# Plain fp32 for the first 36 blocks of U, GpSimd's low parts of U from block 36 on, and one-hots with the expert index innermost

## The reference

```python
q = (xt @ w_q).reshape(n_tok, PEER_HEADS, PEER_DKEY)
s1 = einsum('thd,nd->thn', q[..., :half], sub_k1); s2 = ...   # 128 keys each
v1, i1 = lax.top_k(s1, 16); v2, i2 = lax.top_k(s2, 16)
cand_s = (v1[..., :, None] + v2[..., None, :]); cand_i = i1 * 128 + i2
top_s, pos = lax.top_k(cand_s, 16); idx = take_along_axis(cand_i, pos)
g = softmax(top_s)
u = take(u_tab, idx); act = gelu(einsum('chkd,cd->chk', u, x))
out = einsum('chk,chkd->cd', g * act, take(v_tab, idx))
```

## Time and profile before

| | us |
|---|---|
| median of 3 runs | 2933.95 (2921.36 to 2942.88) |
| the profiled execution | 2944.07, span 2942.2 |
| PE busy | 2668.6 (91%) |
| DVE busy | 1974.5 (67%) |
| POOL busy | 1425.9 (48%) |
| ACT busy | 851.6 (29%) |
| outer products, L903, 2048 records | 934.6 |
| split hidden blocks and queries, L628 to L630 | 2059.3 |
| builds, L886, 3072 records | 281.9 |
| low parts on POOL, L502, 268 | 698.1 |

### The profile page before, as it was taken

How to read it: one execution, slowest core, us unless ns; L and a number is a source line. 1 busy time by engine, 2 the same in 40 slices (tenths; PEclk the granted TensorE clock), 3 DMA queues, 4 the chain that set the end, 5 groups by cost and what they waited for, 6 DMA issues and landing times.

```text
span 2942.2 us, 38986 instructions
## 1 busy us (share of the span) xinstructions
PE 2668.6 (91%) x14882; PEld 1975.3 (67%) x14882; DVE 1974.5 (67%) x3947; ACT 851.6 (29%) x1471; POOL 1425.9 (48%) x840
## 2 busy tenths in 40 slices
PE   6788769988999999999969996999799999999995
PEld 2655559978845577766647665998784456677663
DVE  2446446998657767767663445599875776677666
ACT  2356534442200022222234633354220001222222
POOL 3647545991254434445545803499214443344552
PEclk9899889998999999999979967999899999999998
DMA  6475423774599978889944802377459997788994
GB/s 239 120 162 157 150 65 111 214 240 143 186 395 370 325 276 289 298 316 371 351 147 116 230 8 67 102 203 241 147 161 380 383 322 278 267 312 295 372 359 162
DMA packets 223699, 686.36 MB, mean 233 GB/s; under 512 B 32827, under 2 KB 65995, under 8 KB 223002
## 3 DMA queue, kind: packets, MB, share of 16 engines
q1 hardware_dynamic: 145216, 398.52, 41.2%
q0 software_dynamic: 77728, 284.98, 27.6%
q10 hardware_dynamic: 570, 0.36, 0.0%
HBM read 663.97 MB, written 23.69 MB: 234 GB/s over the span
## 4 chain that ended last, share of the span: by engine, by line
PE 67%; DVE 18%; DMA 9%; POOL 2%; issue 2%; ACT 2%; SPq 0%; ACTq 0%; DVEq 0%; POOLq 0%
PE ps L903 26%; PE ps L886 8%; PE ps L628 8%; PE ps L629 8%; PE ps L630 8%; DMA ring<-in_u 5%; POOL ring_lo L502 2%; DMA ring<-in_v 2%; PE ps L772 2%; DVE arena L1656 2%; PE ps L791 2%; DVE arena L1652 2%; DMA ring<-in_w_mod 1%; DVE ss L1637 1%; DVE arena L1658 1%
## 5 line engine op out<-in xcount | busy, mean ns | idle before, releaser
L903 PE MATMUL ps<-ring,arena 128*128 128x512 f32 x2048 | 934.6, 603 | 13.8 <-DVE arena L1719 10.4
L502 POOL TENSOR_TENSOR ring_lo<-ring,ring_hi 128x1024 fp32r<-128x1024 f32 x268 | 698.1, 2625 | 359.9 <-ACT ring_hi L1021 359.2
L628 PE MATMUL ps<-x_hi,ring_hi 128*128 128x256 f32 (+1 forms) x2304 | 723.9, 314 | 17.0 <-POOL ring_lo L502 8.2
L629 PE MATMUL ps<-x_lo,ring_hi 128*128 128x256 f32 (+1 forms) x2304 | 668.1, 290 | 0.0
L903 PEld LDWEIGHTS ps<-ring,arena 128*128 128x128 f32 x2048 | 380.4, 193 | 427.6 <-issue 407.9
L630 PE MATMUL ps<-x_hi,ring_lo 128*128 128x256 f32 (+1 forms) x2304 | 667.3, 290 | 0.0
L1021 ACT ACTIVATE ring_hi<-ring 128x1024 fp32r<-128x1024 f32 x420 | 442.4, 1057 | 683.7 <-DMA ring<-in_u 546.6
L537 POOL DMA_INDIRECT arena<-in_u_rows,arena x256 | 301.4, 1177 | 562.5 <-DVE arena L1733 530.6
L537 POOL DMA_INDIRECT arena<-in_v,arena x256 | 367.4, 1435 | 421.2 <-DVE arena L1747 327.3
L628 PEld LDWEIGHTS ps<-x_hi,ring_hi 128*128 128x128 f32 x2304 | 444.0, 193 | 54.7 <-issue 38.0
L629 PEld LDWEIGHTS ps<-x_lo,ring_hi 128*128 128x128 f32 x2304 | 444.0, 193 | 28.2 <-issue 28.2
(11 more groups left out here) (210 smaller groups left out, 2648.6 us busy)
## 6 DMA issues: line engine op xcount, KB each, us to landing
ring<-in_u SPq DMA_DIRECT2D x256, 512.0 KB
ring<-in_v SPq DMA_DIRECT2D x256, 512.0 KB
ring<-in_w_mod SPq DMA_DIRECT2D x96, 512.0 KB
ring<-in_w_in SPq DMA_DIRECT2D x36, 512.0 KB
ring<-in_w_q SPq DMA_DIRECT2D x32, 512.0 KB
gelu_half<-arena SPq DMA_DIRECT2D x128, 128.0 KB
arena<-gelu_half SPq DMA_DIRECT2D x128, 128.0 KB
ring<-in_w_out SPq DMA_DIRECT2D x16, 512.0 KB
```

Source lines behind the costliest of these rows:

```text
L502: pool.tensor_tensor(slot_lo[pos], slot[pos], f32(slot_hi[pos]), ALU.subtract).then_inc(lo_done(pos), 1)
L628: mm(out, x[0], y[0], start=first, stop=False, skip_group_check=check)
L629: mm(out, x[0], y[1], start=False, stop=False, skip_group_check=check)
L903: ins = mm(ps[:, t + 3 * q, :], GL[:, b % GLS, P * t - P:P * t], slot[c % RING][:, 512 * q:512 * q + 512], start=(b == 0), stop=(b == KEYS ...
```

## The change

Seven things change together. The first 36 blocks of U are plain fp32 products with the fp32 features as the moving operand and without high or low parts; for that the features of the mixer lie in the arena's rows region, behind the third gather row, and the first three gathers come before, the others after, the wait for block 35. The builds of 64 width start at block 36 instead of 48, so that the blocks 52 to 63 have none. POOL makes the low parts of 36 to 63, with no, one or two gathers between them. DVE makes no low parts before block 64. Its scaled one-hots are written with the expert index innermost, and PE reads them so. DVE does half a dot product a block in 36 to 51 and two in 52 to 63, and the rest by block 64. The sums over V's rows start at block 65 instead of 73. ACT's two exponentials move from blocks 18 and 38 to 12 and 29.

```diff
-PLAIN = SPILL - PAIRS // 2
+PLAIN = 36
+HF_ROW = 3
-POOL_LOWS = 52
...
-            raw.update(range(c0 + SPILL, c0 + 2 * SPILL), ...)
+            raw.update(range(c0, c0 + PLAIN), range(c0 + SPILL, c0 + 2 * SPILL), ...)
...
             def experts(l):          # POOL
                 c0 = start["uv", l]
-                for b in range(RING, 31):
+                pool.wait_ge(sem("p_rows"), l + 1)
+                for r in range(HF_ROW):
+                    gather(l, r)
+                for b in range(PLAIN, PLAIN + RING):
                     low(c0 + b)
-                pool.wait_ge(sem("p_rows"), l + 1)
-                for b in range(31, POOL_LOWS):
-                    if b - 31 < ROWS:
-                        gather(l, b - 31)
+                pool.wait_ge(used((c0 + PLAIN - 1) % RING), turn_of(c0 + PLAIN - 1))
+                for r in range(HF_ROW, ROWS):
+                    gather(l, r)
+                r = ROWS
+                for b in range(PLAIN + RING, SPILL):
                     low(c0 + b)
+                    for _ in range(2 if 2 * (b - RING - PLAIN) >= PAIRS else b % 2):
+                        gather(l, r)
+                        r += 1
...
-                    ob = OB[...].rearrange("p j (e t) -> p j e t", e=width)     # PE, build
+                    ob = OB[...].rearrange("p j (t e) -> p j t e", e=width)
...
-                            ins = mm(..., OA[:, p % 2, :, t], ob[:, j, :, t],
+                            ins = mm(..., OA[:, p % 2, :, t], ob[:, j, t, :],
...
-                    columns_of(u_chunk(l, b), ps[:, bank, 0:STOK], P)           # PE, hidden
+                    if b >= PLAIN:
+                        columns_of(u_chunk(l, b), ps[:, bank, 0:STOK], P)
+                        return
+                    c = u_chunk(l, b)
+                    wait_loaded(pe, c)
+                    for k in range(KC):
+                        ins = mm(ps[:, bank, 0:STOK], slot[c % RING][:, P * k:P * k + P], HFS[1][:, k, P:],
+                                 start=(k == 0), stop=(k == KC - 1))
+                    ins.then_inc(used(c % RING), 1)
...
-                    tt(ob[:, 0], e2, it(2, width), ALU.mult)                    # DVE, one_hots
-                    tt(ob[:, 1], e2, it(3, width), ALU.mult).then_inc(sem("oh_ready"), 1)
+                    ev = e2.rearrange("p e t -> p t e")
+                    for j in range(2):
+                        ins = tt(ob[:, j], ev, IT16[:, 2 + j, col:col + PIECE].unsqueeze(2)
+                                 .to_broadcast([P, PIECE, width]), ALU.mult)
+                    ins.then_inc(sem("oh_ready"), 1)
...
                 for b in range(PLAIN, SPILL):                                   # DVE, experts
-                    one_hots(2 * (b - PLAIN))
-                    one_hots(2 * (b - PLAIN) + 1)
-                    if b + RING < SPILL:
-                        low(u_chunk(l, b + RING))
-                    dot(dots)
-                    dots += 1
+                    more = 2 * (b - PLAIN) < PAIRS
+                    if more:
+                        one_hots(2 * (b - PLAIN))
+                        one_hots(2 * (b - PLAIN) + 1)
+                    for _ in range(b % 2 if more else 2):
+                        dot(dots)
+                        dots += 1
...
-                    if b == SPILL + 9:
+                    if b == SPILL + 1:
                         weigh()
-                    while b >= SPILL + 9 and sums < P and 54 * sums < P * (b - SPILL - 8):
+                    while b >= SPILL + 1 and sums < P and 62 * sums < P * (b - SPILL):
```

More of the change, by code:

```diff
@@ L208, in build @@
         Xv = X[:, :].rearrange("p (t d) -> p t d", t=NT)
-        HF = ar(0, KC * TOK).rearrange("p (k t) -> p k t", k=KC)
+        HFS = [ar(at, KC * TOK).rearrange("p (k t) -> p k t", k=KC) for at in (0, Q_ROWS + HF_ROW * D)]
         xh = x_hi[:, :].rearrange("p (k t) -> p k t", k=KC)
@@ L284, in build @@
             c0 = start["uv", l]
-            raw.update(range(c0 + SPILL, c0 + 2 * SPILL), range(c0 + 130, c0 + 256, 2), (c0 + 255,))
+            raw.update(range(c0, c0 + PLAIN), range(c0 + SPILL, c0 + 2 * SPILL), range(c0 + 130, c0 + 256, 2), (c0 + 255,))
         split_turns, counts = [], [0] * RING
@@ L507, in split @@
                 for c in range(first, min(last, total)):
-                    low(c)
+                    if c not in raw:
+                        low(c)
             def ahead(stage, first=0, last=None):
@@ L518, in features @@
                     r = slice(P * t, P * t + P)
-                    pool.tensor_tensor(xl[:, 4:8, r], HF[:, 4:8, r], f32(xh[:, 4:8, r]), ALU.subtract
+                    pool.tensor_tensor(xl[:, 4:8, r], HFS[n % 2][:, 4:8, r], f32(xh[:, 4:8, r]), ALU.subtract
                                        ).then_inc(sem("xlo_pool"), 1)
@@ L912, in experts @@
                     hidden(b, 6 + b % 2)
-                    build(2 * (b - PLAIN))
-                    build(2 * (b - PLAIN) + 1)
+                    if 2 * (b - PLAIN) < PAIRS:
+                        build(2 * (b - PLAIN))
+                        build(2 * (b - PLAIN) + 1)
                 pe.wait_ge(sem("it_ready"), since("it_ready", l) + 3)
@@ L1025, in done @@
                 act.wait_ge(used(c % RING), turn_of(c))
-                if c + RING < total:
+                if c + RING < total and c + RING not in raw:
                     high(c + RING)
@@ L1046, in features @@
                     for k in range(4):
-                        ins = fn(HF[:, 4 + k, r], ps[:, 2 * t + 1, P * k:P * k + P], ACT.Identity,
+                        ins = fn(HFS[w][:, 4 + k, r], ps[:, 2 * t + 1, P * k:P * k + P], ACT.Identity,
                                  scale=modv[:, l, 3 * w + 1, 4 + k, COND[t]:COND[t] + 1],
@@ L1051, in features @@
                     act.wait_ge(sem("h_act"), since("h_act", n) + t + 1)
-                    fn(xh[:, 4:8, r], HF[:, 4:8, r], ACT.Copy).then_inc(sem("xhi_act"), 1)
+                    fn(xh[:, 4:8, r], HFS[w][:, 4:8, r], ACT.Copy).then_inc(sem("xhi_act"), 1)
             def gate_row(n, m, bank):
@@ L1351, in features @@
                     link(ins)
-                    link(dve.tensor_copy(xh[:, 0:4, r], HF[:, 0:4, r]))
-                    tt(xl[:, 0:4, r], HF[:, 0:4, r], f32(xh[:, 0:4, r]), ALU.subtract).then_inc(sem("xlo_dve"), 1)
+                    link(dve.tensor_copy(xh[:, 0:4, r], HFS[w][:, 0:4, r]))
+                    tt(xl[:, 0:4, r], HFS[w][:, 0:4, r], f32(xh[:, 0:4, r]), ALU.subtract).then_inc(sem("xlo_dve"), 1)
             def diagonals(n):
@@ L1752, in experts @@
                 for b in range(PLAIN, SPILL):
-                    one_hots(2 * (b - PLAIN))
-                    one_hots(2 * (b - PLAIN) + 1)
-                    if b + RING < SPILL:
-                        low(u_chunk(l, b + RING))
-                    dot(dots)
-                    dots += 1
+                    more = 2 * (b - PLAIN) < PAIRS
[5 more added lines that the diff above has]
+                        dots += 1
+                early = dots
                 dve.wait_ge(sem("g_ready"), since("g_ready", l) + PAIRS)
@@ L1765, in experts @@
                         one_hots(PAIRS + b + 1 - QUARTER)
-                    for _ in range(2 - b % 2):
+                    while dots < early + (P - early) * (b + 1) // SPILL:
                         dot(dots)
                         dots += 1
+                dve.wait_ge(sem("row_used"), at["row_used"] + P)
+                dve.tensor_copy(ss[:, 25:26], HSEL[:, P - 1:P]).then_inc(sem("p_dots"), 1)
                 for b in (SPILL, SPILL + 1):
@@ L1782, in experts @@
                         diagonals(2 * l + 1)
-                    if dots < P:
-                        for _ in range(2):
-                            dot(dots)
-                            dots += 1
-                        if dots == P:
-                            dve.wait_ge(sem("row_used"), at["row_used"] + P)
-                            dve.tensor_copy(ss[:, 25:26], HSEL[:, P - 1:P]).then_inc(sem("p_dots"), 1)
-                    if b == SPILL + 9:
+                    if b == SPILL + 1:
                         weigh()
-                    while b >= SPILL + 9 and sums < P and 54 * sums < P * (b - SPILL - 8):
+                    while b >= SPILL + 1 and sums < P and 62 * sums < P * (b - SPILL):
                         accumulate(sums)
```

25 lines of the change are left out of this document (14 added, 11 removed).

## The result

| | before | after |
|---|---|---|
| median of 4 runs, same chip | 2935.98 us (2921.36 to 2942.88) | 3023.51 us (3015.12 to 3038.59) |
| span of the profiled execution | 2942.2 | 3013.3 |
| PE busy | 2668.6 | 2658.8 |
| DVE busy | 1974.5 | 2084.8 |
| POOL busy | 1425.9 | 1302.5 |

The change makes the kernel slower, by a ratio of 1.0308 (95% interval 1.0277 to 1.0339), which is 88 us. The forecast's own range ended at 3010 and did not hold the time; the wider span over all rivals ended at 3035.

What follows compares the result with a forecast made beforehand. PE was taken as the bound except in each layer's DVE-bound retrieval. Picks 37 us earlier, then DVE-bound builds and POOL-paced blocks, put the first outer product 22 us later; two layers, 44 to 45 us on 2934, give 2979, range 2955 to 3010.

Steps and rivals of the forecast that it cites:

- Plain blocks and picks: Blocks 0 to 35: 3.49 us each on PE; without POOL's lock DVE done at 623, picks at 636, gain 37 us.
- Start of the one-hots: Hand-over from picks to builds: one-hots start 2.8 us after the picks.
- The failed step: the scaled one-hots: Blocks 36 to 51: DVE's strided, broadcast-innermost read adds 0.27 us per instruction, making a pair 2.32 us.
- rival 3: Blocks 36 to 51: lock holds and DVE's strided read costs 0.98; 8.8 us a block, 3028 us; chance 0.08.
- The lock on f16 instructions: Blocks 36 to 51: each POOL low part costs DVE 2.1 us, making a block 7.35 us.
- rival 1: Blocks 36 to 51: POOL's lows don't hold f16 instructions back; DVE block 5.25 us, 2902 us; chance 0.20.
- rival 2: Blocks 36 to 51: lock holds but scaled one-hots keep their speed; block 6.3 us, 2944 us; chance 0.12.
- Builds: PE's 64-column products fall from 0.123 to 0.064 us each; the 32-column builds of later stages gain nothing.
- rival 4: Weight load isn't the 32-column builds' limit: 38 us a layer saved, 2902; chance 0.08, with POOL's lock absent 2826, 0.07.
- rival 5: Layout doesn't speed 64-column products, PE 6.8 a block, forecast unmoved; PE clock drop up to +25 a layer; within forecast's 0.45.
- Blocks 52 to 63 and the hand-over: POOL's low part and two gathers take 5.3 us; twelve blocks 47.4; last gelu to first outer product stays 6.4.
- The outer products: Blocks 0 to 95 behind the first outer product: no change, PE paces and covers DVE's extra 0.27 us a build.

Runs made afterwards that it cites:

- Experiment 3: Changed kernel, scaled one-hots reading the match table in memory order, still written expert index innermost (wrong table values): 2990.38 us, ratio 1.02.
- experiment 4: Changed kernel, POOL's low parts of blocks 40 to 63 cut from 1024 to 16 columns: 2930.45 us, ratio 0.9992 to the kernel before.
- experiment 1: Changed kernel with the one-hot layout undone, piece innermost again in DVE's writing and PE's reading: 2963.88 us, ratio 1.0117 to the kernel before.
- experiments 4 and 5: The second of these: changed kernel with low parts of blocks 40 to 63 made by DVE, none by POOL: 2965.86 us, ratio 1.0126.
- experiment 7: Changed kernel with V's sums started at block 73 and spread over 54 blocks, as before the change: 3035.76 us, ratio 1.0331.
- experiment 6: Changed kernel with low parts of blocks 40 to 63 on DVE and scaled one-hots piece innermost again, leaving plain blocks: 2952.33 us, ratio 1.0064.

## Why the prediction was right and wrong, step by step

**Plain blocks and picks: right.** Forecast 3.49 us for a block, DVE done at 623 and the picks at 636; measured 3.52, 623.9 and 633.6. DVE's 128x2048 instructions all take 2.29 us now. The account of POOL's lock on the retrieval held to 1 us.

**Start of the one-hots: 5 us off.** I gave 2.8 us from picks to one-hots, it took 8.2. Some 4 us of the difference are ACT's, which comes to the picks behind a high part that waited for its chunk. The other 1.4 are the lock again: DVE's conversion at 639.60 takes 1.72 us where it took 0.29 before, and POOL's low part beside it (638.82, 2.35 us) ends at 641.17. With the earlier picks it left +3.

**The failed step: the scaled one-hots.** "I take 0.27, because those f32 inputs are the nearest case of one element at a time." The term was 0.27 us for each of four instructions of a block; measured is 0.63, half of the difference between a pair of 3.04 us and one of 1.78. Experiment 3, whose pair is 2.27 us, splits it: 0.25 for the broadcast innermost, nearly as taken, and 0.38 for the stride of 16 bytes, which the f32 rows had not. A block is 8.61 us (17.22 for two) instead of 7.35, sixteen of them 20 us more, and as the stage was DVE's, all of it counted. That was rival 3's read (1.0 against its 0.98), with a chance of 0.08. That rival 3's 3028 us comes within 5 of the measured time is luck in part: it had the read and the block right (8.8), but neither the 14 us a layer that came on top nor the 33 us that the outer products and the stretch between the layers took off. The prediction had both conditions in hand and took only one: the read broke the doubled rate and also stepped from line to line, and the row it took as nearest shared the first condition alone. A nearest row must be near in every property that the change alters. Of the Trainium skill's two pages named there, VectorE: DVE Perf Modes (section "What auto-detection actually checks") grants two results a cycle only with step 1, and the trace agrees with 0.34 to 0.60 us. SBUF — State Buffer (section "Specifications (TRN2)") has a penalty for each cross to a new 16-byte line and gives no figure for it; 0.60 to 1.0 us is the size measured with such a step, and whether that penalty is the cause no run shows.

**The lock on f16 instructions: right.** Forecast 2.1 us a low part, measured 2.05. It is the larger part of the loss (93 us go with the low parts in experiment 4, 60 with the layout in experiment 1; the two overlap). Rivals 1 and 2 fall: rival 1 by experiments 4 and 5, rival 2 by experiment 1's block against the change's.

**Builds.** The 64-wide products fell to 0.062 us (16 in 1.0), forecast 0.064. The 3072 products of all widths, 281.9 us busy before, take 216.3; of the 66 us less, 7 are the 2048 of width 32 (151.3 before, 143.9 after), so rival 4 falls. The time saved on PE was worth nothing: PE then waited for L1727, and the chip granted less than full speed.

The prediction named such a clock in rival 5 and put it at nothing. In the stages with and without builds the granted clock is 0.79 and 0.81, where it was 0.96. Two products of the split block from PE's timeline, the first at 2.4 GHz; the second, at 1.2 GHz, comes behind waits of 7.51 and 4.44 us:

```profile
636.90 0.28 PE L637 MATMUL ps<-x_lo,ring_hi 128*128 128x256 f32 x1
...
644.82 1.18 PE L894 MATMUL ps<-arena 128*128 128x64 f16 x16 [7.51 <-DVE arena L1727]
650.43 1.19 PE L894 MATMUL ps<-arena 128*128 128x64 f16 x16 [4.44 <-DVE arena L1727]
...
652.01 0.41 PE L638 MATMUL ps<-x_hi,ring_lo 128*128 128x256 f32 x1
```

In the changed kernel it costs nothing that the runs can show, as DVE sets the pace there.

**Blocks 52 to 63 and the hand-over: small, same sign.** POOL's low part with two gathers takes 5.76 us (784.66 to 824.98 for seven), forecast 5.3, and the twelve blocks 51.9 instead of 47.4. From the last gelu (831.98) to the first outer product (842.47) it is 10.5 us, forecast 6.4 "and stays". The DMA engines are full there, 397 GB/s at a busy share of 1.02 from 832 to 842.4 us, where before it was 176 and 0.59 (782 to 788.8): store and fetch share them with chunks and gathered rows. That this is why they are late is read from these windows, not tested.

Together in layer 0: 2.4 early at the picks, 5.4 late to the one-hots, 19.7 from the blocks, 4.5 and 4.1: the first outer product at 842.5, where I had 811. In layer 1 it comes at 2281.4 against 2195.4.

**The outer products: forecast no change, measured less.** From the first to the last outer product before and after it is 709.8 and 700.7 us in layer 0, 716.0 and 701.6 in layer 1. It takes back 9 + 14 of the loss. The layout alone does as much (701.2 and 703.2), but the kernel with the layout undone does too (702.7 and 705.2), and with the sums put back it is 704.7 and 705.6. So more than one part gives it, and they don't add up. About half is time in which PE stood still (6.1 and 10.8 us before, 2.7 and 2.2 after, for ACT's evictions and DVE's products mainly); why these waits went stays open. Another 10 us of the span lie between the layers. From the last outer product of layer 0 to the first hidden block of layer 1 the changed kernel takes 404.5 us, the kernel before 414.4 and experiment 7, the same there as the changed one, 420.1. As above, they go with the granted clock (0.88, 0.85 and 0.85), so I read nothing into them.

**The sum**: 53.7 in layer 0, 51.4 in layer 1 (2281.4 - 1947.6 from the first hidden block, before 2195.4 - 1913.0), less 23.5 and 10 is 72 of the span, 71.1 measured; the medians differ by 88, since the profiled execution of before was 8 us above its median of this comparison and that of the change 8 below. Two errors of the forecast partly cancel: the layers lost some 60 us more than it had, and the outer products and the stretch between the layers gave 33 back that it hadn't.

## What to carry to other kernels

A layout that makes one engine's read contiguous is paid by the one that writes it: price the write's inputs by each property that changes (rate of two a cycle, stride in bytes), and by a row that shares all of them. Work moved to GpSimd isn't beside VectorE's, if both have two inputs in SBUF: here a low part cost VectorE 2.05 us on GpSimd and 1.13 on VectorE itself. And before a stage's work is moved past a hand-over, ask what is spent behind it: 36 us won ahead of the picks went into 12 blocks of 37.7 us behind them. And before two profiled spans are compared, look at a stretch that is the same in both: here such a stretch alone differed by up to 22 us, with the granted clock.

## What the runs showed of the hardware that had not been expected

- VectorE, two f16 inputs in SBUF, 512 elements from start to start: 0.34 us with the broadcast in the middle, 0.60 with it innermost, 1.0 with a stride of 16 bytes as well.
- The wait for GpSimd's TENSOR_TENSOR is the same for f16 instructions as for f32 ones. In experiment 3 the pair of 1.28 us becomes 3.49 beside a low part.
- Stores are paid late: with gelus 2.88 us apart ten of the twelve late blocks in experiment 6 don't wait for a store, the last two wait 4.04 and 4.08 us.
